# Raw and split weight pieces at 4 and 4 in place of 6 and 3, with the dense loop written out

## What is computed

```python
for i in range(DEPTH):                                   # DEPTH = 2
    a = hybrid_mixer(rmsnorm(h), w_in[i], ..., w_out[i]) # stick-breaking + forgetting attention + pooling
    h = h + rmsnorm(a)
    c = memory_cross_attention(rmsnorm(h), rmsnorm(mem), xa_wq[i], xa_wkv[i], xa_wo[i])
    h = h + rmsnorm(c)
    hn = rmsnorm(h)
    if i % 2 == 0:
        f = (silu(hn @ w_gate) * (hn @ w_up)) @ w_down   # dense, 1024 x 2816
    else:
        f = top-2-of-8 routed experts, each with its own w_gate, w_up (1024 x 2816), w_down (2816 x 1024)
    h = h + rmsnorm(f)
```

## Time and profile before

| | |
|---|---|
| Median of 3 runs | 1686.45 us (1684.34 to 1688.24) |
| Profiled execution | 1683.32 us |
| Its span, first to last instruction | 1681.5 us |
| PE, DVE, ACT busy | 1534.2, 1105.6, 945.2 us |
| TensorE's granted clock, mean | 0.968 |
| Moved by DMA | 385.73 MB, mean 229 GB/s |

### The profile page before, as it was taken

One profiled execution on the slowest core, in us unless ns is written; L12 is line 12 of the kernel. 1 busy time (PEld: TensorE's weight loads), 2 busy tenths in 40 slices (PEclk: granted clock), 3 DMA queues, 4 the chain that ended last, 5 costly groups with the idle time before them and its releaser, 6 DMA issues.

```text
span 1681.5 us, 23033 instructions
## 1 busy us (share of the span) xinstructions
PE 1534.2 (91%) x9287; PEld 1315.7 (78%) x9287; DVE 1105.6 (66%) x1037; ACT 945.2 (56%) x1017; POOL 152.3 (9%) x129
## 2 busy tenths in 40 slices
PE   6989987999979999976999998998999899999986
PEld 5969977999959789866999766676766799966664
DVE  4556545444455546543777788888888677678887
ACT  4355435333443555342545687887878544578785
POOL 7100000000013000003000102020030200010200
PEclk9989998999989899996999999999999999999999
DMA  9308522555533075420667799999999766689994
GB/s 312 105 7 282 189 101 101 175 175 179 191 117 126 1 238 188 151 88 27 238 223 247 278 371 363 349 384 334 378 354 374 280 212 243 239 284 376 364 370 166
DMA packets 223987, 385.73 MB, mean 229 GB/s; under 512 B 11893, under 2 KB 114521, under 8 KB 223721
## 3 DMA queue, kind: packets, MB, share of 16 engines
q1 hardware_dynamic: 223048, 382.16, 65.1%
q0 software_dynamic: 512, 0.74, 0.2%
q10 hardware_dynamic: 288, 1.05, 0.2%
HBM read 382.85 MB, written 1.05 MB: 228 GB/s over the span
## 4 chain that ended last, share of the span: by engine, by line
PE 75%; DVE 13%; ACT 7%; issue 4%; DMA 1%; SPq 0%; DVEq 0%; ACTq 0%
PE banks L1534 12%; PE banks L1535 12%; PE banks L1536 12%; DVE w_low L1125 9%; PE banks L1532 8%; PE banks L1533 7%; PE banks L1850 6%; PE banks L1852 5%; ACT w_high L724 5%; PE banks L1786 2%; PE banks L1794 2%; PE banks L1745 1%; PE banks L1552 1%; PE banks L1731 1%; PE banks L1944 1%
## 5 line engine op out<-in xcount | busy, mean ns | idle before, releaser
L1125 DVE TENSOR_TENSOR w_low<-raw,w_high 128x2048 fp32r<-128x2048 f32 x357 | 808.4, 2294 | 299.0 <-ACT w_high L724 293.2
L724 ACT ACTIVATE w_high<-raw 128x2048 fp32r<-128x2048 f32 x357 | 679.4, 1914 | 265.6 <-PE banks L1852 100.9
L1532 PE MATMUL banks<-w_high,rows 128*128 128x512 f32 (+1 forms) x576 | 224.1, 395 | 24.2 <-DVE w_low L1125 23.5
L1534 PE MATMUL banks<-w_high,rows 128*128 128x256 f32 x832 | 237.6, 286 | 5.1 <-DVE rows L1125 2.8
L1535 PE MATMUL banks<-w_low,rows 128*128 128x256 f32 x832 | 235.9, 283 | 0.0
L1536 PE MATMUL banks<-w_high,rows 128*128 128x256 f32 x832 | 235.8, 283 | 0.0
L1533 PE MATMUL banks<-w_low,rows 128*128 128x512 f32 (+1 forms) x576 | 212.9, 376 | 0.7 <-issue 0.7
L1850 PE MATMUL banks<-rows,w_high 128*128 128x320 f32 x704 | 186.3, 310 | 7.5 <-issue 6.2
L1852 PE MATMUL banks<-rows,w_low 128*128 128x256 f32 x704 | 184.5, 279 | 0.0
L1534 PEld LDWEIGHTS banks<-w_high,rows 128*128 128x128 f32 x832 | 160.1, 192 | 6.6 <-DVE rows L1125 3.6
L1532 PE MATMUL banks<-w_high,eT 128*128 128x512 f32 x352 | 144.2, 410 | 20.2 <-DVE w_low L1125 13.5
(11 more groups left out here) (186 smaller groups left out, 2077.4 us busy)
## 6 DMA issues: line engine op xcount, KB each, us to landing
raw<-in_moe_w_gate_dram SPq DMA_DIRECT2D x176, 512.0 KB, 5.5
raw<-in_moe_w_up_dram SPq DMA_DIRECT2D x176, 512.0 KB, 5.4
raw<-in_moe_w_down_dram SPq DMA_DIRECT2D x176, 512.0 KB, 5.3
raw<-in_w_in_dram SPq DMA_DIRECT2D x40, 512.0 KB, 5.9
raw<-in_xa_wkv_dram SPq DMA_DIRECT2D x32, 512.0 KB, 8.9
raw<-in_dense_w_gate_dram SPq DMA_DIRECT2D x22, 512.0 KB, 4.4
raw<-in_dense_w_up_dram SPq DMA_DIRECT2D x22, 512.0 KB, 4.1
raw<-in_dense_w_down_dram SPq DMA_DIRECT2D x22, 512.0 KB, 3.6
```

Source lines behind the costliest of these rows:

```text
L724: return act.activation(out_, in_, ACT.Copy, scale=scale)
L1125: return dve.tensor_tensor(out_, in_, plain(high), ALU.subtract)
L1532: pe.matmul(dst, stay[0], move[0], start=start, stop=False, skip_group_check=True)
L1534: pe.matmul(dst, stay[0], move[0], start=start, stop=False, skip_group_check=True)
```

## The change

RAW goes from 6 to 4 and SPLIT from 3 to 4, in the same memory (96 KB of each partition). Eight pieces have room in place of nine. SP's load of piece c now waits for the low part of c - 4 instead of c - 6, and the split of c for PE's end of c - 4 instead of c - 3; each `ahead(c)` now splits one piece further. The dense loops relied on slots that repeat every six pieces, and are written out.

```diff
-RAW = 6
-SPLIT = 3
+RAW = 4
+SPLIT = 4
...
                 gate_up(ws, c, r, 0)
-                with sp.Fori(0, (STEPS - 1) // 2) as n:
-                    for j in range(2):
-                        gate_up(ws, c + 2 + 3 * j, r + n, n * (2 * FFC) + (j + 1) * FFC)
-                        down(ws, c + 4 + 3 * j, r + n, n * (2 * FFC) + j * FFC)
+                for n in range(1, STEPS):
+                    gate_up(ws, c + 3 * n - 1, r, n * FFC)
+                    down(ws, c + 3 * n + 1, r, (n - 1) * FFC)
                 down(ws, c + MIXER - 1, r, (STEPS - 1) * FFC)
...
-                with act.Fori(0, (STEPS - 3) // 2) as k:
-                    for j in range(2):
-                        step(layer, c + 5 + 3 * j, k, k * 2 + (2 + j), 2)
+                for n in range(2, STEPS - 1):
+                    step(layer, c + 3 * n - 1, 0, n, 2)
...
-                with dve.Fori(0, (STEPS - 3) // 2) as k:
-                    for j in range(2):
-                        step(layer, c + 5 + 3 * j, k, k * 2 + (2 + j), 2)
+                for n in range(2, STEPS - 1):
+                    step(layer, c + 3 * n - 1, 0, n, 2)
...
-                    gate_or_up(c, 0, 0, turned=0)
-                    gate_or_up(c + 1, 1, 1)
+                    gate_or_up(c, c % SPLIT, 0, turned=0)
+                    gate_or_up(c + 1, (c + 1) % SPLIT, 1)
                     turn_hidden(0)
-                    step(c + 2, 2, 1, begin=True)
-                    with pe.Fori(0, STEPS - 2) as i:
-                        step(i * 3 + (c + 5), 2, i + 2)
-                    down(c + MIXER - 1, 2, STEPS - 1)
+                    for n in range(1, STEPS):
+                        step(c + 3 * n - 1, (c + 3 * n - 1) % SPLIT, n, begin=(n == 1))
+                    down(c + MIXER - 1, (c + MIXER - 1) % SPLIT, STEPS - 1)
```

## The result

The changed kernel is slower. Its median is 1695.46 us (5 runs, 1690.45 to 1698.26) beside 1686.45 us (1684.11 to 1688.24) for the kernel before on the same chip; the ratio is 1.0043, with a 95% interval of 1.0027 to 1.0059. A second measurement gave 1696.11 us and 1.0076 (1.0054 to 1.0098). The forecast was 1675 us, 10.7 us faster. 1695 us lies in its range, on the other side of no change. The profiled execution took 1695.46 us, 12.1 us more than that of before.

What follows compares the result with a forecast made beforehand. PE was taken to bound all but the six narrow experts (571.4 us), where splits and DMA matter. There 574.2 us for 198 pieces, less 21.5 from store, plus 8 gave 560.7, so about 1675 us; range 1654 to 1712 us.

Steps and rivals of the forecast that it cites:

- The store: Behind a wide expert all eight slots are full; 3.7 pieces each at experts 1 and 6 save 21.5 us.
- The written-out loop, "0": Dense step: PE is busy throughout, back edge included, so writing out the loop wins back nothing, 0 us.
- t = 2.9 us and 8 us at the changes: Narrow experts: time t per piece with four raw slots; DMA runs dry some 2 us at each of four expert changes.
- One split further ahead: Narrow experts: D0's split leaves the ring; with endless supply a step takes 15.5 us, an expert 90.7 in place of 96.5.
- (1): Narrow steps: PE's waits for L1125 end with ACT waiting for a DMA into raw, not for PE.
- (2): Full narrow steps last 17 to 17.5 us once the store is used up; experts 1 and 6 are shortest, near 91 us.
- (3): Narrow experts: a DMA's median time to landing falls from 6.9 to about 5.5 us.
- (4): Change of experts: PE's wait of 2.91 us for the low part is gone.
- (5): Projections, dense and wide stretches keep their lengths within 1 us each.
- DVE's floor: Narrow experts: six at 90.7 us, 544 us together, set by DVE's own work; given as the range's lower end.
- Supply starves: Raw ring in narrow steps: the change loses above t = 2.96 us; at 3.1 us +27.5 us, about 1713 us; chance 0.31.
- Nothing moves: DMA is already at its limit of about 359 to 362 GB/s, so slot counts don't help; 1683 to 1687 us; chance 0.14.

Runs made afterwards that it cites:

- h44: The changed kernel with every load of the experts' weights moving half of its elements; 1625.37 us, ratio 0.9657 to the kernel before.
- x54: The changed kernel with a fifth raw piece in attention scratch memory while the experts run, two small tiles moved; 1670.35 us, ratio 0.9898 to the kernel before.

## Why the prediction was wrong

*The store: the step that failed.* "Against this stands a store ... So 3.7 pieces each time are drawn from store, at experts 1 and 6", worth 21.5 us. It gave next to nothing. Without it the sum reads 198 x 2.9 + 8 = 582.2 us, and the trace has 581.8. (The second profile of the same kernel has 578.0, so the agreement within a microsecond is partly luck.) Experts 1 and 6 should have been the shortest, near 91 us; they took 96.3 and 99.3, beside 97.5, 97.2 and 97.1 for experts 2 to 4 (96.5 and 98.4 in the second profile, beside 96.2, 97.6 and 95.4). The reason stands in the row 932.49:961.76. For the first ten pieces of expert 1 TensorE is busy for 29.27 of 29.27 us, 2.93 us a piece, with h44's half supply as with the full (29.30 of 29.30). It doesn't go faster than t there even with ample supply, so nothing is drawn that shortens anything. Meanwhile DMA moved only 279 GB/s, 8.2 MB or 7.8 pieces in place of the ten that were used: raw slots came free only with splits, and these waited for TensorE. When the full steps begin, where TensorE could use pieces faster than 2.9 us, 2.2 of the 3.7 pieces have gone, unused. Even with ample supply expert 1 is no shorter than the others (86.4 beside 85.8 and 84.9 us in h44). The count of 3.7 pieces is shaky too: (6.6 + 4.2 + 0.5)/2.9 is 3.9, which leaves 0.4 of a piece for TensorE in the 4.3, where its 2.1 us a piece would make 0.7.

*The written-out loop, "0".* Right where it looked: seven dense steps take 122.7 us before and after. Wrong for the kernel: 4 to 5 us, at a branch 850 us later. The prediction asked what the back edges cost, not what longer code does to other branches; the 6.22 us stood in the trace of before.

*t = 2.9 us and 8 us at the changes.* Together 33 x 2.9 + 2 = 97.7 us for an expert; measured 97.5, 97.2, 97.1. The mechanism and the mean size were right (96.2, 97.6 and 95.4 in the second profile), the place was not. Counted from its first matmul, expert 2 goes in parts of 29.9, 16.2, 16.8, 17.8 and 16.8 us (its start, three full steps, and the last step with the change to expert 3's body), where the kernel before has 32.1, 17.5, 16.5, 16.5 and 13.8. It gains 3.5 us in the first two parts and loses 4.6 us in the last three. Full steps run at 2.7 to 3.0 us a piece, and the largest loss, 3.0 us, stands in the last step. Its break-even of 2.96 us, store and all, needed the store; without it the change loses at any t above (571.4 - 8)/198 = 2.85 us. That is the true margin, and the prediction's own t lay above it.

*One split further ahead.* Floor of 90.7 us with endless supply: it is 85 to 86. The term was undersized by 5 us: the full steps of h44 last 14.6 to 15.0 us in place of 15.5, and what is left of an expert beside four of them is some 27 us in place of 28.7. The 5 us more played no part here, since supply bound first.

*What the profile would show.* (1) Right: ACT waits for landings. (2) Partly right for the full steps (those of expert 2 take 16.2, 16.8 and 17.8 us), wrong for experts 1 and 6. (3) Wrong: in the two windows of rows 8 and 9 the medians are 6.0 and 6.2 us, from 5.1 and 6.9: the late one fell by half as much as forecast, the early one rose. (4) Half right: the 2.91 us are gone, but a wait of 1.65 us has come one piece later, and the change of experts went from 31.59 us to 30.77. (5) Right, as far as it was measured (dense steps, wide expert 0), except expert 5, 1.3 us longer.

*The range.* Its lower end is called DVE's floor at 1654 us, but the sum with that floor of 544 us gives 1656 us, or 1659 for a median; the four chances add up to 1, so nothing is left for the 0.15 to 0.2 said to lie outside.

*The rivals.* "Supply starves" is what happened, at a smaller t than it named (2.96 with the pauses, not 3.1) and through the missing store. "Nothing moves" is out: x54 moved 385 GB/s for a whole expert. The Trainium skill ("DMA: Bandwidth & Descriptors", specifications) has about 358 GB/s from HBM for one core, which by the same page is the share when both cores of a pair stream; here one core runs. 377 and 385 GB/s over 92.7 and 91.1 us lie above that figure, and the measurement decides.

## What to carry to other kernels

Two kinds of buffer slots are not interchangeable: a split slot lowers the floor of the engines, a raw slot keeps the queues full, and halving the bytes moved shows in one run which of the two binds. Here six raw pieces were one more than three splits could use, and four were one too few; the fifth (5 and 4) beat the kernel before by 1.0% and the changed one by 1.4 to 1.8%, and the room for it lay in memory that another stage had left. Don't credit a full buffer as time: it shortens only a stretch in which the consumer could go faster than the supply, and only if it is still full when that stretch begins. And cost a written-out loop not at its own back edges alone but also at the data-dependent branches behind it: here one of them took 4 to 7 us more.

## What was not expected of the hardware

TensorE stands 6.2 us at the branch into a body of other code, and 10 to 13 us when one loop 850 us earlier is written out, with no releaser in the profile; the longer stand has one more 16 KB packet of instructions in it. With the weight traffic halved it is 4.7 and 5.6 us. DMA reads 385 GB/s on one core for 91 us on end when five raw slots are open, and 357 to 362 GB/s when four are, from the same queues and in the same sizes.
